# Expert blocks numbered by expert, and the second block's gate and up weights loaded into places of their own

## The reference

```
lg = xt @ w_rg + b_rg;  g_idx = argmax(lg);  g_prob = softmax(lg)[g_idx]
le = (xt @ w_re + b_re) of group g_idx;  top_l, top_i = top_k(le, 2);  top_p = softmax(top_l)
expert = g_idx * 8 + top_i;   weight = g_prob * top_p          # 2048 (token, expert) pairs
out[token] += weight * ((silu(x @ w_gate[e]) * (x @ w_up[e])) @ w_down[e])
```

## Time and profile before

| what | value |
|---|---|
| median of 3 runs | 1697.09 us (1693.78 to 1698.38) |
| the profiled execution: its time, its span | 1697.08 us, 1695.4 us |
| PE busy, DVE busy, ACT busy, POOL busy | 93%, 80%, 41%, 22% |
| moved by DMA | 351.80 MB, mean 208 GB/s |
| `e_raw` loads: gate, up, down | x132, x132, x66 |
| the chain that ended last | PE 61%, DMA 18%, DVE 12%, ACT 4%, issue 3% |

### The profile page before, as it was taken

How to read it: one execution, slowest core, us unless ns; L and a number is a source line. 1 busy time by engine, 2 the same in 40 slices (tenths; PEclk the granted TensorE clock), 3 DMA queues, 4 the chain that set the end, 5 groups by cost and what they waited for, 6 DMA issues and landing times.

```text
span 1695.4 us, 21361 instructions
## 1 busy us (share of the span) xinstructions
PE 1571.0 (93%) x7056; PEld 1286.6 (76%) x7056; DVE 1358.5 (80%) x1145; ACT 695.9 (41%) x584; POOL 366.8 (22%) x219
## 2 busy tenths in 40 slices
PE   2799999999999999999999946999999999999985
PEld 2588888888888888778878835888887777777774
DVE  5777878697877877987464467999999988899996
ACT  4401011211201112345131135677776766666773
POOL 1101000000000010000000002455444544445451
PEclk9999999999999999999999958999999999999997
DMA  7424223232314224535454248999999999999964
GB/s 258 143 63 136 73 101 111 79 116 77 111 62 136 78 96 132 183 118 163 149 178 137 94 155 298 353 365 372 376 361 350 356 357 363 355 352 355 370 200 170
DMA packets 167145, 351.80 MB, mean 208 GB/s; under 512 B 16882, under 2 KB 90610, under 8 KB 167109
## 3 DMA queue, kind: packets, MB, share of 16 engines
q1 hardware_dynamic: 150838, 309.71, 51.7%
q0 software_dynamic: 16272, 41.62, 8.1%
HBM read 323.31 MB, written 45.61 MB: 218 GB/s over the span
## 4 chain that ended last, share of the span: by engine, by line
PE 61%; DMA 18%; DVE 12%; ACT 4%; issue 3%; POOL 1%; DVEq 0%; SPq 0%; POOLq 0%; ACTq 0%
PE ps L1429 19%; PE ps L1431 19%; PE ps L1430 19%; DMA e_raw<-in_w_down_dram 16%; DVE e_lo L1314 3%; ACT e_hi L822 2%; DVE e_lo L1310 2%; DMA xg<-d_h,g_idx 1%; DVE conv_acc_b L1062 1%; DVE macc L968 1%; PE ps L1566 1%; PE ps L1618 1%; DVE B_lo L1147 1%; DVE xnT L955 0%; DMA prow<-in_c_dram 0%
## 5 line engine op out<-in xcount | busy, mean ns | idle before, releaser
L1429 PE MATMUL ps<-A_hi,w_hi 128*128 128x512 f32 x1024 | 400.2, 391 | 5.2 <-DVE A_lo L998 5.2
L1431 PE MATMUL ps<-A_hi,w_lo 128*128 128x512 f32 x1024 | 398.9, 390 | 0.0
L1430 PE MATMUL ps<-A_lo,w_hi 128*128 128x512 f32 x1024 | 398.9, 390 | 0.0
L1310 DVE TENSOR_TENSOR e_lo<-e_raw,e_hi 128x2048 fp32r<-128x2048 f32 x136 | 309.2, 2286 | 11.8 <-ACT e_hi L816 10.6
L1062 DVE SCALAR_TENSOR_TENSOR conv_acc_b<-glu,colc,conv_acc_b 128x1024 f32<-128x1024 f32 x232 | 298.0, 1284 | 10.2 <-DVE rows L1047 0.5
L816 ACT CAST e_hi<-e_raw 128x2048 fp32r<-128x2048 f32 x136 | 259.7, 1912 | 59.2 <-PE ps L1431 53.8
L1429 PEld LDWEIGHTS ps<-A_hi,w_hi 128*128 128x128 f32 x1024 | 192.6, 188 | 46.9 <-issue 4.4
L1430 PEld LDWEIGHTS ps<-A_lo,w_hi 128*128 128x128 f32 x1024 | 192.6, 188 | 40.4 <-issue 0.5
L1431 PEld LDWEIGHTS ps<-A_hi,w_lo 128*128 128x128 f32 x1024 | 192.5, 188 | 40.1
L1429 PE MATMUL ps<-e_hi,xT_hi 128*128 128x512 f32 x528 | 212.4, 402 | 0.0
L1431 PE MATMUL ps<-e_hi,xT_lo 128*128 128x512 f32 x528 | 206.7, 391 | 0.0
(11 more groups left out here) (270 smaller groups left out, 2093.9 us busy)
## 6 DMA issues: line engine op xcount, KB each, us to landing
e_raw<-in_w_gate_dram SPq DMA_DIRECT2D x132, 512.0 KB, 6.0
e_raw<-in_w_up_dram SPq DMA_DIRECT2D x132, 512.0 KB, 12.5
e_raw<-in_w_down_dram SPq DMA_DIRECT2D x66, 1024.0 KB, 14.0
w_raw<-in_w_in_dram SPq DMA_DIRECT2D x56, 512.0 KB, 4.2
stream<-in_w_ada_dram SPq DMA_DIRECT2D x48, 512.0 KB, 5.5
xn<-in_x_dram SPq DMA_DIRECT2D x8, 512.0 KB, 7.0
d_short<-conv_acc_a POOLq DMA_DIRECT2D x8, 512.0 KB, 4.0
d_gate_a<-gate_st POOLq DMA_DIRECT2D x8, 512.0 KB, 2.9
```

Source lines behind the costliest of these rows:

```text
L1310: v.tensor_tensor(e_lo[:, q, :], e_raw[:, q, :], e_hi[:, q, :].bitcast(F32), ALU.subtract).then_inc(gu_lo, 1)
L1429: t.matmul(dst, st_hi, mv_hi, start=first, stop=False)
L1430: t.matmul(dst, st_hi, mv_lo, start=False, stop=False)
L1431: return t.matmul(dst, st_lo, mv_hi, start=False, stop=last)
```

## The change

- Block e, for e from 0 to 31, is now the first 128 rows of expert e. Further rows of any expert go into blocks 32 and on, in order of expert. So the experts of blocks 0 to 31 are known without the table. The number of blocks is 32 plus the number of further blocks.
- SP loads gate and up of block 1 (expert 1) right behind the loads of block 0, into four places `park[q]`, each free at its time: 0 and 1 in B_hi, 3 in two rows of `rows` (after the last h2), 2 over `h2` and the router's weights (after the last logits and the last store of h2).
- The loads that go out when block 0's pieces have been split (`gu_lo` 1 to 4) are now those of block 2, into `e_raw`. SP's loop starts at b = 1.
- Parks 1 and 2 lie in places of down's `e_hi` and `e_lo`. ACT therefore waits for `gu_lo` before it copies block 0's down pieces, and DVE before it subtracts them.
- DVE subtracts all four pieces of block 0 before `x_lo(0)`.
- Routing computes block numbers in the new way: the expert's number (`own`), the rank's block and row before the starts are known, and five instructions over 16 columns that choose between own block and further block. Three pairs of multiply and reduce over [128, 2, 8, 32] (`of_pair`) take the place of one multiply-add and two such pairs over [128, 8, 32].
- POOL fills three more small tables before the first store of x1. `iota_t` and `oh_prev` change places in `rows`, and the row of g_final with them. Eight semaphores are shared by the x rows, w_o and the parked pieces.

```diff
-        big = rt("big", [P, NT, NE])
+        big = rt("big", [P, 2, NT, NE])
...
+        park = [at("park0", (NCH + 4) * 4 * C8, [P, C8], F32), at("park1", (NCH + 5) * 4 * C8, [P, C8], F32),
+                at("park2", (2 * NCH + 5) * 4 * C8, [P, C8], F32), at("park3", oR + SH2 * T4, [P, C8], F32)]
...
+        x_full = [sem(f"rows_full{i}") for i in range(NT)]
+        wo_full, park_full = x_full[0:4], x_full[4:8]
...
-            def load_gu(q, e):
+            def load_gu(q, e, parked=False):
                 for part, w in ((0, w_gate), (1, w_up)):
-                    dst = e_raw[:, q, part * D:(part + 1) * D].rearrange("p (k n) -> p k n", k=2)
+                    raw = park[q] if parked else e_raw[:, q, :]
+                    dst = raw[:, part * D:(part + 1) * D].rearrange("p (k n) -> p k n", k=2)
...
                 load_down(q, 0)
-            sp.wait_ge(s_tab, 1)
-            n_blk = sp.value_load(tab[0:1, NBLK:NBLK + 1], min_val=PAIRS // P, max_val=NBLK - 1)
-            e_one = sp.value_load(tab[0:1, 1:2], min_val=0, max_val=NE - 1)
+            for q in range(2):
+                load_gu(q, 1, True)
+            sp.wait_ge(s_h2, NT)
+            load_gu(3, 1, True)
+            sp.wait_ge(s_lgev, NT)
+            sp.wait_ge(sp_h2, 16 * NT)
+            load_gu(2, 1, True)
             for q in range(4):
                 sp.wait_ge(gu_lo, q + 1)
-                load_gu(q, e_one)
-            with sp.Fori(0, NBLK) as b:
+                load_gu(q, 2)
+            for q in range(2):
+                sp.wait_ge(d_lo, q + 1)
+                load_down(q, 1)
+            sp.wait_ge(s_tab, 1)
+            n_blk = sp.value_load(tab[0:1, NBLK:NBLK + 1], min_val=NE, max_val=NBLK - 1)
+            with sp.Fori(1, NBLK) as b:
...
             for q in range(3):
-                gu_split(q, 64, q + 1)
+                gu_split(q, 48, q + 1, True)
             gate(0, 4, None)
-            gu_split(3, 64, 4)
+            gu_split(3, 48, 4, True)
             for q in range(2):
+                act.wait_ge(gu_lo, 4 + q + 1)
                 d_split(q, 16, None)
...
+            def of_pair(dst, per_expert):
+
+                step(v.tensor_tensor(big[:], e_k[:], per_expert, ALU.mult))
+                step(v.tensor_reduce(dst, big[:], AX_X, ALU.add))
+
+            of_pair(own[:], bc(iota_n[:].unsqueeze(1), both))
             dve.wait_ge(s_rank, 1)
...
             dve.sem_inc(s_nb, 1)

-            dve.wait_ge(s_start, 1)
-            step(v.tensor_copy(cum[:, 0, :], ps[:, 3, 0:NE]))
-            step(v.scalar_tensor_tensor(mask[:], bc(cum[:, 0, :].unsqueeze(1), [P, NT, NE]), float(P),
-                                        ps[:, 0, 0:NT * NE].rearrange("p (i e) -> p i e", i=NT), ALU.mult, ALU.add))
-            for k in range(2):
-                step(v.tensor_tensor(e_k[:, k], e_k[:, k], mask[:], ALU.mult))
-                step(v.tensor_reduce(posf[:, k, :], e_k[:, k], AX_X, ALU.add))
+            rank = ps[:, 0, 0:NT * NE].rearrange("p (i e) -> p i e", i=NT)
+            of_pair(posf[:], bc(rank.unsqueeze(1), both))
             step(v.tensor_copy(posi[:], posf[:]))
...
+            dve.wait_ge(s_start, 1)
+            step(v.tensor_copy(cum[:, 0, :], ps[:, 3, 0:NE]))
+            of_pair(posf[:], bc(cum[:, 0, :].unsqueeze(1).unsqueeze(1), both))
+            step(v.tensor_tensor(posf[:], posf[:], blkf[:], ALU.add))
+            step(v.scalar_tensor_tensor(posf[:], posf[:], float(NE - 1), own[:], ALU.add, ALU.subtract))
+            step(v.tensor_scalar(blkf[:], blkf[:], 1.0, None, ALU.min))
+            step(v.tensor_tensor(posf[:], posf[:], blkf[:], ALU.mult))
+            step(v.tensor_tensor(blkf[:], posf[:], own[:], ALU.add))
...
-            for q in range(2):
+            for q in range(4):
                 gu_split(q, q + 1)
             x_lo(0, 1)
-            for q in range(2, 4):
-                gu_split(q, q + 1)
 
             x_lo(1, 2)
             for q in range(3):
-                gu_split(q, 4 + q + 1)
+                gu_split(q, 4 + q + 1, True)
             hidden(0, 1)
-            gu_split(3, 8)
+            gu_split(3, 8, True)
+            dve.wait_ge(gu_lo, 8)
```

More of the change, by code:

```diff
@@ L197, in encoder_block @@
         blk_i = rt("blk_i", [P, 2, NT], I32)
+        own = rt("own", [P, 2, NT])
         blkf = rt("blkf", [P, 2, NT])
@@ L284, in encoder_block @@
         s_ohi, s_olo = sem("wo_hi"), sem("wo_lo")
[L285 removed]
+        s_bk = sem("last_out_slab_k")
         pe_o, s_x1, s_ss3, s_h2 = sem("pe_o"), sem("x1_ready"), sem("ssq3"), sem("h2_ready")
@@ L810, in _, with gu_split @@
             a.activation(act_warm[:], ident[:, 0:1], ACT.Sigmoid).then_inc(s_warm, 1)
-            def gu_split(q, full, before):
-                act.wait_ge(e_full[q], full)
+            def gu_split(q, full, before, parked=False):
+                act.wait_ge((park_full if parked else e_full)[q], full)
                 if before is not None:
                     act.wait_ge(gu_used, before)
-                a.copy(e_hi[:, q, :], e_raw[:, q, :]).then_inc(gu_hi, 1)
+                a.copy(e_hi[:, q, :], park[q][:] if parked else e_raw[:, q, :]).then_inc(gu_hi, 1)
             def d_split(q, full, before):
```

58 lines of the change are left out of this document (33 added, 25 removed).

## The result

The changed kernel takes 1700.53 us (median of 14 runs, 1698.59 to 1703.17) against 1698.21 us (14 runs) for the kernel before: a ratio of 1.0022, with a 95% interval of 1.0014 to 1.003. By the ratio, which the text goes by, that is +3.7 us, 2.4 to 5.1; the two medians lie 2.3 us apart. It is within 0.3%, as forecast, and inside the range; of the +1.4 us forecast the sign and the place were right, the size was not. The profiled execution has a span of 1699.3 us against 1695.4, +3.9, so the pair of traces can be read for the difference.

The account below looks back on a forecast made before the run. Late expert stage bound by weight loads (DMA), early one by PE and DVE; 1697.08 + 0.9 (routing) + 1.0 (gather of block 1) - 0.5 (backlog) = 1698.5 us, range 1691.5 to 1703.5.

Parts of the forecast that it names:

- What bounds the kernel: Late expert stage waits for weights, early one is held by PE and DVE; ahead lies a 26 us DMA hole.
- Parked loads: Start of expert stage: the 11.7 us of loads fill the first hole, a second of some 17 us opens; -0.5 us.
- term of -0.5 us for a backlog: At block 3's first load, 1055.27: fewer bytes issued and not landed, -0.5 us, bounds -2.4 and 0.
- Routing: DVE in routing: `own` covered by idle time, the longer work behind it adds 0.9 us, bounds 0 and +1.9.
- The splits ahead of `x_lo(0)`: DVE's four splits hold POOL, block 1's gather lands later and PE waits for it: +1.0 us, bounds 0 and +3.7.
- rival B: POOL held by the splits, block 1's gather at its upper bound, PE's clock rises later: 1704.4 us, chance 0.11.
- upper bound for the gather: Block 1's gather: POOL's copy takes a full 2.4 us, issue at 1024.1, landing at 1033.1, +3.7 us.
- The new waits, the table's read, the last blocks: ACT's and DVE's waits for `gu_lo`, SP's table read (up to 1 us), moved expert rows: 0 taken.
- Rival A: Late stage bound by bytes, lead kept: 11.7 us sooner, 1687.3 us; chance 0.14 in full or by more than a third.
- Rival C: Parked loads collide with routing, last store of h2 holds DVE: 2 us if last in line, 1700.5 us; chance 0.07.
- signs named for being wrong: Block 3 goes out clearly before 1055, exposed down-weight waits (from about 1220) start later, or the mixer's end moves.

Follow-up runs that it names:

- run 2: The changed kernel without the parked loads, block 1 loaded into `e_raw` when block 0's pieces are split: 1700.31 us, 1.0017 of the kernel before.
- run 4: The kernel before without block 1's gate/up loads (the block uses what lies in `e_raw`): 1694.21 us, 0.9983 of the kernel before.
- Run 3: The kernel before without block 14's gate/up loads (the block uses what lies in `e_raw`): 1691.00 us, 0.996 of the kernel before.
- run 9: The changed kernel without parks and with the old order of splits, leaving the new numbering and routing: 1696.88 us, 1.0002 of the kernel before.
- run 6: The changed kernel with block 2's loads held until both gathers have landed, four splits kept: 1697.21 us, 0.9999 of the kernel before.
- run 10: The kernel before with block 1's loads held until both gathers have landed, nothing else: 1695.89 us, 0.9996 of the kernel before.
- run 8: Early start: the kernel before, block 1's loads held until both gathers landed, block 0's splits and down copies rearranged: 1691.35 us, 0.9966 (-5.8 us).
- run 5: The kernel before with all four pieces of block 0 subtracted ahead of `x_lo(0)`: 1697.97 us, 1.0002 of the kernel before.
- run 11: The changed kernel, unaltered, measured once more: 1701.67 us, 1.0024 of the kernel before.

## Why the prediction was right, and where its sizes were off

- **What bounds the kernel, and "Parked loads":** right. The second hole came where it was put (some 1035 to 1054 but for a gather, forecast 1033 to 1050), there was no place for block 3, and runs 2 and 4 show that the bytes of block 1 are worth nothing early beyond what they do to the gather. Run 3 shows why the stage table misleads: the same bytes are worth 6.8 us where DMA is the last to come. The term of -0.5 us for a backlog bought nothing: block 3's loads land after 4.0 us at least, 4.9 in the middle, against 4.0 and 4.7.

```profile
DMA to landing us min/median/max: 4.0/4.9/7.0
```

- **"Routing", +0.9:** 1.02 in the trace. An instruction over 512 columns took 0.69 us and 0.72 from start to start, as the step from 256 to 384 columns gave, and `own` cost nothing under its cover. By time alone (run 9) it can't be told from 0.
- **"The splits ahead of `x_lo(0)`", +1.0:** the right mechanism, somewhat too small: 1.32 in the trace. POOL was held as computed (2.21 against 2.4, issue at 1022.3 + 0.8 for the later start), and the landing was the one of full queues, 8.4 us against 8.5, not 6.6 + 1.3; run 6 shows that it is the weight loads beside the gather that make it so.
- **The mis-sized step is that sum, +0.9 + 1.0 - 0.5 where 3.7 was measured.** It counted no clock behind the gather; the later rise of the clock stood in rival B alone. PE waited 1.8 us longer ahead of its second transposes (4.26 against 2.45), the rise of the clock came later behind PE's start, which cost 0.84 us, and turn 1 took 1.10 more. With these, and the 0.70 of the mixer, the early stage is 5.4 us late. That 1.85 of it comes back in the late stage had not been counted either. 1.02 + 1.32 + 0.84 - 0 = 3.2 would have been the better sum up to turn 0. That the total came out within 2.3 us of the forecast is thus partly luck: the clock's 1.9 us and the late stage's -1.85, both uncounted, cancel.
- **A slip in the upper bound for the gather:** a full copy of 2.4 us from 1020.2 on puts the issue at 1020.2 + 2.4 + 0.9 = 1023.5 and not at 1024.1, so the bound is +3.1 and not +3.7, and the range's upper end some 0.6 lower. The measured time lies inside either.
- **The new waits, the table's read, the last blocks, 0:** no cost of them shows in the trace. The down loads of block 1 and block 3's first piece lie 5.75 us apart, 5.54 before.
- **Rival A** fell in full: in the changed kernel, and in run 4, where block 1's bytes are gone altogether. **Rival B** was its direction, at a third of its price on POOL: the copy began in the middle of the second split and took 1.25 us to its end, not 2.4. **Rival C** fell: the last store of h2 had landed by 987.7, when POOL, which waits for it, goes on, and from 990 to 1013.4 DVE has no idle time over 0.41 us ahead of an instruction.
- **Two of the signs named for being wrong did show.** The mixer's end moved, by 0.70 to 0.93 us; over all the traces that is scatter (see behind the table). And the exposed waits for down weights started later, at 1270.99 and not at 1210.92:

```profile
1210.92 1.91 ACT L822 CAST e_hi<-e_raw 128x2048 fp32r<-128x2048 f32 x1 [1.04 <-DMA e_raw<-in_w_down_dram]
```

```profile
1270.99 1.92 ACT L843 CAST e_hi<-e_raw 128x2048 fp32r<-128x2048 f32 x1 [1.30 <-DMA e_raw<-in_w_down_dram]
```

That looks like a lead kept in part, but it doesn't tell: the kernel before with a hold and no parks (run 10) has its first at 1262.93, runs with parks lie from 1210.71 to 1270.99, and those without from 1186.37 to 1262.93 (a single one at 1059.00 in run 8 left aside). A part of rival A of 1 or 2 us is not excluded by this; run 2's time, 1.0017 without the parks against 1.0022 and 1.0024 with them, gives no sign of one.

- **What stays open:** the order of the splits costs 0.3 and 1.5 us on the kernel before, but undoing it in the changed kernel is worth about 3.4 (1.0022 against 1.0002). The new routing alone costs 0.3. The parts don't add up to 3.7; the differences are about as large as the intervals. The traces show where a difference could come from, not why: between turns 10 and 31 run 5 made up 3.0 us, the changed kernel 1.85 in one execution and nothing in another (run 11), and run 9 lost 1.25 more.

## What to carry over

A hole in DMA's timeline is worth its bytes only if a free buffer lets the lead last until the stage that waits for bytes: ask where the next load but one will go, before moving one. Where it can't last, look at the first load that has no place until the engines make one: in the changed kernel block 3's piece went out 4.0 us later and the end came 3.9 us later, and in the early start 4.1 sooner and 5.8. It is a guide and no law: in run 5 the piece went out 3.1 us later, that trace ended 2.5 later, and over twelve executions the kernel was 0.3 slower, which can't be told from nothing. When VectorE's work is moved beside GpSimd's gathers, or loads beside a gather's bytes, the gather pays, and where PE waits for it, TensorE's clock adds to it.
